# One-hots of the second key on GpSimd, low halves of the gated tiles on VectorE

## The chip, the cores and the metric

The kernel runs on one core of a Trainium2 chip, in one launch. The metric is the time of one execution on the device in microseconds. A profile of one execution shows every instruction of the core's engines: TensorE (PE, and PEld for its weight loads), VectorE (DVE), ScalarE (ACT), GpSimd (POOL) and SyncE (SP), which issues the large transfers.

## What is computed

A network of two blocks in float32 over 256 tokens of 1024 features. The first block (mLSTM, retention, a feed-forward part) and the mixers of the second aren't touched by the change. The change lies in the second block's two PEER layers, cut here to what matters:

```python
q = (x @ w_q).reshape(B, T, PEER_HEADS, 2, PEER_DKEY // 2)
s = jnp.einsum('bthcd,hcnd->bthcn', q, sub_keys)           # 8 heads, 2 sub-keys of 128 each
top_s, top_i = lax.top_k(s, PEER_TOPK)                     # 16 of each
cand_s = top_s[..., 0, :, None] + top_s[..., 1, None, :]
cand_i = top_i[..., 0, :, None] * 128 + top_i[..., 1, None, :]
best_s, pos = lax.top_k(cand_s, PEER_TOPK)
idx = jnp.take_along_axis(cand_i, pos, axis=-1)            # one of 128 x 128 experts
gate = jax.nn.softmax(best_s, axis=-1)
...
h = jax.nn.gelu(jnp.einsum('md,mkd->mk', xb, exp_u[ib]), approximate=False)
return jnp.einsum('mk,mkd->md', gb * h, exp_v[ib])
```

Each token thus picks 8 x 16 = 128 experts (i, j) with a gate each.

## The kernel before

**Dense experts.** The kernel doesn't gather. It computes the hidden value of all 16384 experts for all 256 tokens, multiplies it with a gate that is zero for the experts not chosen, and multiplies by all of `exp_v`. The weights stream through as tiles of 128 x 2048 float32 (1 MB): a "hidden" tile p holds `exp_u` of two values of j with all 128 values of i on the partitions, an "output" tile `exp_v` of two values of j. There are 64 of each per layer. Hidden tiles 0 to 47 come first, then 16 output tiles, then the rest.

**High and low halves.** float32 products are made of three matmuls of a faster type: high x high, high x low, low x high. For each tile ScalarE makes `w_hi` (line 1902), and VectorE (`split_lo`, line 2167) or GpSimd (`lo`, line 1479) makes `w_lo`, the raw tile less `w_hi`. TensorE's `hidden(p)` runs 16 units of three matmuls (lines 1787 to 1789) on a tile. There are two buffers of w_hi and w_lo (three in the first 21 tiles of a layer), so `w_hi` of tile p + 2 waits until TensorE is through with tile p, and `w_lo` follows it. The set `LO_BY_POOL` says which tiles are GpSimd's: 2 to 24, and then every other one from 27 to 47. SP loads tile k when `w_lo` of tile k - 4 is done.

**Gates.** From tile 25 to tile 46 TensorE also makes the gates, in 64 groups of GT = 4 tokens per layer, three groups in a tile (behind units 4, 9 and 15; in tiles 25 and 46 two). For one token the gate matrix over (i, j) is a product of two one-hot matrices with the 128 choices on the partitions: `hot_i` (choice by i) and `hot_j` (choice by j), the latter weighted with the gate value. `gates(g)` (line 1770) runs four such matmuls into one of five PSUM banks. `ijg` holds, with the choices on the partitions, the key i (row 0), the key j (row 1) and the gate value (row 2) of each token. The iota 0 to 127 lies in bank 0 of PSUM for VectorE, and among the constants in SBUF as `cst("iota")`. `hot_i` and `hot_j` have HOT = 3 buffers each.

**Order of the work around the change, written out by hand.** VectorE's `one_hot(g)` (line 2480) compares the iota with `ijg` for four tokens at once, first into `hot_j`, then into `hot_i`, and raises `hot_eq`. GpSimd's `weigh(g)` (line 1484) waits for `hot_eq`, multiplies `hot_j` in place with the gate values and raises `hot_ready`, for which TensorE waits. When a group's gates are there (`gates_done`), VectorE's `apply(g)` (line 2490) multiplies them into the hidden values `hid` of the tiles before, and then calls `one_hot(g + 3)`. ScalarE copies the rest of the gates to `hid` and `staged` (lines 2064, 2068) and raises `gates_read`. In hidden tile n VectorE's queue is: `apply` of the groups in mid-tile, `split_lo(n + 2)` unless GpSimd has it, line 2505 (hidden values of tile n times the gates that are already there), `apply` of the group at the end. GpSimd's queue has for each group of tile p the weighing of three groups ahead, and behind the first of them `lo(p + 1)` if it is its tile. Both engines work strictly in the order of their queues.

Of the kernel before, what the change touches and what calls it, by code (L numbers as in the profile page):

```python
# [9 lines left out]
ALU = mybir.AluOpType  # L10
# [3 lines left out]
P = 128  # L14
# [177 lines left out]

LO_BY_POOL = set(range(2, 25)) | set(range(27, HELD, 2))
LO_COUNT = {}
_counts = {True: 0, False: LAYERS * TILES_A}
for _t in range(TILES_B):
# [998 lines left out]
def second_block(nc, ctx, m, base, erows, ecols, lora_w, side_w, keys, ln_rows, consts_b, spill, out):  # L1198
# [256 lines left out]
    @block.gpsimd  # L1455
    def _(pool):
        pool.dma_start(side_raw[:, :, :], side_w).then_inc(side_loaded, 16)
        pool.dma_start(const_even[:, :], consts_b[:, 0:CONST_EVEN]).then_inc(b_const, 16)
        pool.dma_start(const_rest[:, :], consts_b[:, CONST_EVEN:CONSTS_B]).then_inc(b_const, 16)
        pool.dma_start(lora[:, :], lora_w).then_inc(even_loaded, 16)  # L1460
        pool.dma_start(ecol[:, :], ecols).then_inc(even_loaded, 16)
        pool.dma_start(erow[:, :], erows.partition_broadcast(P)).then_inc(even_loaded, 16)

        def ln_load(n):
            pool.dma_start(ln_rows_at[n][:, 0, :], ln_rows[2 * n].partition_broadcast(P)).then_inc(ln_loaded, 16)
            pool.dma_start(ln_rows_at[n][:, 1, :], ln_rows[2 * n + 1].partition_broadcast(P)).then_inc(ln_loaded, 16)

        pool.wait_ge(tr_lo, 8)
        ln_load(0)
        pool.dma_start(keys_sb, keys[0]).then_inc(keys_loaded, 16)  # L1470

        def peer_layer(layer):

            first, g0 = base + PEER_UV[layer], GROUPS * layer

            def lo(q):
                k = first + q
                pool.wait_ge(hi_ready, k + 1)
                nc.gpsimd.tensor_tensor(lo_of(k), raw[:, k % RAW, :], hi_of(k).bitcast(F32), ALU.subtract).then_inc(lo_pool, 1)  # L1479

            def weigh(g):
                pool.wait_ge(hot_eq, g0 + g + 1)
                at = hot_j[:, g % HOT, :, :]
                nc.gpsimd.tensor_tensor(at, at, ijg[:, 2, g * GT:(g + 1) * GT].unsqueeze(2).broadcast_to([P, GT, KEYS]), ALU.mult).then_inc(hot_ready, 1)  # L1484

            for q in range(FIRST_GATED):
                if q in LO_BY_POOL:
                    lo(q)
            for g in range(HOT):
                weigh(g)  # L1490
            for p in range(FIRST_GATED, LAST_GATED + 1):
                for n, g in enumerate(mid_groups(p) + end_groups(p)):
                    if g + HOT < GROUPS:
                        weigh(g + HOT)
                    if n == 0 and p + 1 in LO_BY_POOL:
                        lo(p + 1)
            pool.wait_ge(gates_done, GROUPS * (layer + 1))
            for b in range(2):
                pool.wait_ge(spilled[b], 16 * (SETS // 2) * (layer + 1))
            ln_load(2 * layer + 1)  # L1500

        peer_layer(0)
        pool.wait_ge(x_ready, normed(1, TT - 1))
        ln_load(2)
        pool.wait_ge(att_lo, 2)
        pool.dma_start(keys_sb, keys[1]).then_inc(keys_loaded, 16)
        peer_layer(1)


    @block.tensor  # L1510
    def _(pe):
# [237 lines left out]
        def peer_layer(layer, split):  # L1749
            transposes(x, 2 * layer)  # L1750
            featured(f"pq{layer}", 0, split=split)
            featured(f"pq{layer}", 1)
            pe.wait_ge(keys_loaded, 16 * (layer + 1))
            wait_read(pe, CHUNK_B[f"pq{layer}", 1])
            for t in range(TT):
                for h in range(PH):
                    last = mm(psum[4 * (1 - t) + h // 2][:, (h % 2) * 2 * KEYS:(h % 2 + 1) * 2 * KEYS], pq[:, h, HALVES[t]], keys_sb[:, h, :],
                              start=True, stop=True)
                last.then_inc(s_done, 1)
            pe.wait_ge(s_read, 2 * layer + 1)  # L1760
            tile, g0, p0, w0 = base + PEER_UV[layer], GROUPS * layer, EXPERT_PAIRS * layer, len(WEIGHED) * layer

            def gates(g):

                pe.wait_ge(hot_ready, g0 + g + 1)
                if g >= len(GATE_BANKS):
                    pe.wait_ge(gates_read, g0 + g + 1 - len(GATE_BANKS))
                dst = psum[GATE_BANKS[g % len(GATE_BANKS)]][:, :].rearrange("p (j t) -> p j t", t=GT)
                for i in range(GT):
                    last = mm(dst[:, :, i], hot_i[:, g % HOT, i, :], hot_j[:, g % HOT, i, :], start=True, stop=True)  # L1770
                last.then_inc(gates_done, 1)

            def hidden(p):

                k = tile + hidden_at(p)
                wait_lo(pe, k)
                if p - 2 in WEIGHED:
                    pe.wait_ge(weighed, w0 + WEIGHED.index(p - 2) + 1)
                elif p > 1:
                    pe.wait_ge(gelu_ready, p0 + p - 1)  # L1780
                wh, wl = hi_of(k), lo_of(k)
                after = dict(GROUPS_IN.get(p, ()))
                for jj in range(2):
                    dst = psum[4 + p % 2][:, jj * S:(jj + 1) * S]
                    for kk_ in range(KD):
                        ws = slice((2 * kk_ + jj) * P, (2 * kk_ + jj + 1) * P)
                        mm(dst, wh[:, ws], act_hi[:, kk_, :], start=kk_ == 0 and jj == 0, stop=False)  # L1787
                        mm(dst, wh[:, ws], act_lo[:, kk_, :], start=False, stop=False)  # L1788
                        last = mm(dst, wl[:, ws], act_hi[:, kk_, :], start=False, stop=kk_ == KD - 1 and jj == 1)  # L1789
                        unit = jj * KD + kk_  # L1790
                        if unit == UNITS - 1:
                            last.then_inc(tile_used, 1)
                        if unit in after:
                            gates(after[unit])

            def output(o):

                k = tile + output_at(o)
                begin, end = o == 0, o == EXPERT_PAIRS - 1
                wait_lo(pe, k)  # L1800
                pe.wait_ge(c_lo_ready, p0 + o + 1)
                wh, wl = hi_of(k), lo_of(k)
                for t in range(TT):
                    for jj in range(2):
                        cs = slice(jj * S + t * P, jj * S + (t + 1) * P)
                        for c in range(2):
                            dst, ws = psum[2 * t + c][:, :], slice(jj * D + c * CW, jj * D + (c + 1) * CW)
                            mm(dst, c_hi[:, o % 2, cs], wh[:, ws], start=begin and jj == 0, stop=False)  # L1808
                            mm(dst, c_hi[:, o % 2, cs], wl[:, ws], start=False, stop=False)  # L1809
                            last = mm(dst, c_lo[:, o % 2, cs], wh[:, ws], start=False, stop=end and jj == 1)  # L1810
                    if end and t == 0:
                        last.then_inc(half_done, 1)
                last.then_inc(tile_used, 1)

            for p in range(HELD):
                hidden(p)
                if p == SELECTED:
                    for t in range(TT):
                        pe.wait_ge(sel_ready, 2 * layer + t + 1)
                        for n in range(3):  # L1820
                            last = nc.tensor.transpose(psum[6 + t][:, n * P:(n + 1) * P], sel[:, t, n, :], ident)
                        last.then_inc(sel_t, 1)
                    pe.wait_ge(ijg_ready, 2 * layer + 2)
                    pe.wait_ge(s_read, 2 * layer + 2)
            pe.wait_ge(gates_read, g0 + GROUPS)
            for o in range(EARLY):
                output(o)
            for p in range(HELD, EXPERT_PAIRS):
                hidden(p)
            for o in range(EARLY, EXPERT_PAIRS):  # L1830
                output(o)
# [325 lines left out]
    def _(dve):  # L2157
# [260 lines left out]
        def peer_layer(layer, t0):  # L2418
# [55 lines left out]
            def one_hot(g):  # L2474
# [1 line left out]
                if g >= HOT:  # L2476
                    dve.wait_ge(gates_done, g0 + g + 1 - HOT)
                tok = slice(g * GT, (g + 1) * GT)
                for keys_at, dst in ((1, hot_j), (0, hot_i)):
                    ins = V.tensor_tensor(dst[:, g % HOT, :, :], bcast(psum[0][:, 0:KEYS].unsqueeze(1), [P, GT, KEYS]),  # L2480
                                          bcast(ijg[:, keys_at, tok].unsqueeze(2), [P, GT, KEYS]), ALU.is_equal)
                ins.then_inc(hot_eq, 1)

            def apply(g):

# [347 lines left out]
```

## Time and profile before

| | |
|---|---|
| median of 3 runs | 3635.1 us (3630.31 to 3638.41) |
| the profiled execution's own time | 3633.8 us |
| its span in the profile | 3632.0 us |
| TensorE matmul busy | 3286.6 us (90%) |
| VectorE busy | 2188.9 us (60%) |
| ScalarE busy | 1503.1 us (41%) |
| GpSimd busy | 535.3 us (15%) |
| mean granted TensorE clock | 0.943 |

The gated tiles lie at about 1897 to 2123 us (first PEER layer) and 2941 to 3164 us (second). Times in the trace are microseconds from the start of the span; the busy time of an engine is the sum of its instructions' times, and "idle before, <-releaser" is how long the engine stood still before an instruction and what ended that. The granted clock is TensorE's, as a share of 2.4 GHz.

### The profile page before, as it was taken

To read this page: it belongs to the slowest core of one execution; us is meant where nothing else is said; L and a number is where in the kernel's file an instruction comes from. 1 tells how busy PE (TensorE), PEld (TensorE's weight loads), DVE (VectorE), ACT (ScalarE), POOL (GpSimd) and SP (SyncE) were. 2 spreads that over 40 slices of the span, in tenths; PEclk is the share of its full clock that TensorE was granted. 3 is DMA by queue.
4 is the path that set the end of the run, shared out by engine and by line. 5 is a ranking of instruction groups with operands and counts; after the bars stand their busy time and mean duration, and the time that the engine had idled before them with its cause. 6 is when DMAs were issued, how large, how long until landed. Compare 5 with 4: busy or idle time off the path is not lost.

```text
span 3632.0 us, 49546 instructions
## 1 busy us (share of the span) xinstructions
PE 3286.6 (90%) x20440; PEld 2901.1 (80%) x20440; DVE 2188.9 (60%) x3110; ACT 1503.1 (41%) x1681; POOL 535.3 (15%) x275
## 2 busy tenths in 40 slices
PE   6899999799998998777998899999848988999998
PEld 6787789587877986666998889888638988889886
DVE  4766655566665554745786655555665966654555
ACT  5443444453444444401434344444334443344443
POOL 0000000000000000000566620000001856500000
PEclk9999999889999998877999999999969999999999
DMA  4444545334545553202443355555403533465553
GB/s 181 152 174 170 204 153 186 139 119 160 194 159 174 183 185 145 96 2 71 169 157 121 122 201 206 186 188 191 164 35 135 185 131 112 157 233 184 188 185 127
DMA packets 87677, 565.23 MB, mean 156 GB/s; under 512 B 10176, under 2 KB 10192, under 8 KB 23584
## 3 DMA queue, kind: packets, MB, share of 16 engines
q1 hardware_dynamic: 80496, 534.81, 40.8%
q0 software_dynamic: 6960, 27.27, 2.2%
q8 instruction: 163, 2.67, 0.3%
q14 instruction: 58, 0.48, 0.0%
HBM read 552.61 MB, written 9.44 MB: 155 GB/s over the span
## 4 chain that ended last, share of the span: by engine, by line
PE 43%; DVE 4%; POOL 4%; ACT 3%; issue 1%; ACTq 0%; DVEq 0%
PE bank L1810 7%; PE bank L1808 6%; PE bank L1809 6%; PE bank L1787 6%; PE bank L1788 6%; PE bank L1789 6%; POOL w_lo L1479 3%; ACT w_hi L1902 2%; PE bank L1770 1%; PE bank L1534 1%; PE bank L1535 1%; PE bank L1536 1%; DVE hot_i L2480 1%; POOL hot_j L1484 1%; DVE hot_j L2480 1%
## 5 line engine op out<-in xcount | busy, mean ns | idle before, releaser
L1902 ACT ACTIVATE w_hi<-raw 128x2048 fp32r<-128x2048 f32 x290 | 555.5, 1916 | 844.2 <-PE bank L1810 395.5
L2167 DVE TENSOR_TENSOR w_lo<-raw,w_hi 128x2048 fp32r<-128x2048 f32 x222 | 531.7, 2396 | 614.2 <-ACT w_hi L1902 614.0
L874 DVE TENSOR_TENSOR w_lo<-raw,w_hi 128x2048 fp32r<-128x2048 f32 x202 | 462.6, 2292 | 409.7 <-ACT w_hi L686 406.0
L1787 PE MATMUL bank<-act_hi,w_hi 128*128 128x256 f32 x2048 | 600.8, 293 | 60.8 <-POOL w_lo L1479 55.2
L686 ACT ACTIVATE w_hi<-raw 128x2048 fp32r<-128x2048 f32 x202 | 386.8, 1916 | 542.9 <-PE bank L463 369.8
L1788 PE MATMUL bank<-act_lo,w_hi 128*128 128x256 f32 x2048 | 588.3, 287 | 0.0
L1789 PE MATMUL bank<-act_hi,w_lo 128*128 128x256 f32 x2048 | 587.4, 287 | 0.0
L1787 PEld LDWEIGHTS bank<-act_hi,w_hi 128*128 128x128 f32 x2048 | 400.8, 196 | 66.4 <-POOL w_lo L1479 60.2
L1808 PE MATMUL bank<-w_hi,c_hi 128*128 128x512 f32 x1024 | 405.0, 396 | 0.0
L1809 PE MATMUL bank<-w_lo,c_hi 128*128 128x512 f32 x1024 | 405.0, 395 | 0.0
L1810 PE MATMUL bank<-w_hi,c_lo 128*128 128x512 f32 x1024 | 405.0, 395 | 0.0
L1788 PEld LDWEIGHTS bank<-act_lo,w_hi 128*128 128x128 f32 x2048 | 401.6, 196 | 0.1
L1789 PEld LDWEIGHTS bank<-act_hi,w_lo 128*128 128x128 f32 x2048 | 401.3, 196 | 0.0
L1479 POOL TENSOR_TENSOR w_lo<-raw,w_hi 128x2048 fp32r<-128x2048 f32 x68 | 322.0, 4739 | 195.9 <-ACT w_hi L1902 195.6
L497 PE MATMUL bank<-act_hi,w_hi 128*128 128x256 f32 x1024 | 297.8, 291 | 14.4 <-DVE act_lo L921 8.5
L498 PE MATMUL bank<-act_lo,w_hi 128*128 128x256 f32 x1024 | 296.0, 289 | 0.0
L499 PE MATMUL bank<-act_hi,w_lo 128*128 128x256 f32 x1024 | 295.6, 289 | 0.0
L461 PE MATMUL bank<-w_hi,act_hi 128*128 128x512 f32 x576 | 236.9, 411 | 26.5 <-DVE w_lo L874 22.3
L462 PE MATMUL bank<-w_lo,act_hi 128*128 128x512 f32 x576 | 230.0, 399 | 0.0
L1810 PEld LDWEIGHTS bank<-w_hi,c_lo 128*128 128x128 f32 x1024 | 192.4, 188 | 46.7
L463 PE MATMUL bank<-w_hi,act_lo 128*128 128x512 f32 x576 | 229.5, 399 | 0.0
L1808 PEld LDWEIGHTS bank<-w_hi,c_hi 128*128 128x128 f32 x1024 | 192.4, 188 | 46.4 <-issue 0.3
(482 smaller groups left out, 5758.2 us busy)
## 6 DMA issues: line engine op xcount, KB each, us to landing
raw<-weights SPq DMA_DIRECT2D x492, 1024.0 KB, 4.8
row<-rows POOLq DMA_DIRECT2D x48, 256.0 KB, 4.0
spill<-staged SPq DMA_DIRECT2D x32, 256.0 KB, 3.9
hid<-spill SPq DMA_DIRECT2D x32, 256.0 KB, 4.8
y<-w_pe POOLq DMA_DIRECT2D x2, 1024.0 KB, 5.1
ln_row_mix<-ln_rows POOLq DMA_DIRECT2D x4, 512.0 KB, 4.6
hid<-keys POOLq DMA_DIRECT2D x2, 1024.0 KB, 6.1
ln_row_ffn<-ln_rows POOLq DMA_DIRECT2D x4, 512.0 KB, 7.3
```

Of the source, the lines that this page charges most:

```text
L497: nc.tensor.matmul(dst, wh, hi[:, ki, :], start=ki == 0 and f % 2 == 0, stop=False)
L686: nc.scalar.activation(w_hi[:, k % SPLIT, :], raw[:, k % RAW, :], ACT.Copy).then_inc(hi_ready, 1)
L874: nc.vector.tensor_tensor(w_lo[:, k % SPLIT, :], raw[:, k % RAW, :], w_hi[:, k % SPLIT, :].bitcast(F32), ALU.subtract).then_inc(lo_ready, 1)
L1479: nc.gpsimd.tensor_tensor(lo_of(k), raw[:, k % RAW, :], hi_of(k).bitcast(F32), ALU.subtract).then_inc(lo_pool, 1)
L1787: mm(dst, wh[:, ws], act_hi[:, kk_, :], start=kk_ == 0 and jj == 0, stop=False)
L1788: mm(dst, wh[:, ws], act_lo[:, kk_, :], start=False, stop=False)
L1789: last = mm(dst, wl[:, ws], act_hi[:, kk_, :], start=False, stop=kk_ == KD - 1 and jj == 1)
L1808: mm(dst, c_hi[:, o % 2, cs], wh[:, ws], start=begin and jj == 0, stop=False)
L1809: mm(dst, c_hi[:, o % 2, cs], wl[:, ws], start=False, stop=False)
L1810: last = mm(dst, c_lo[:, o % 2, cs], wh[:, ws], start=False, stop=end and jj == 1)
L1902: A.activation(hi_of(k), raw[:, k % RAW, :], ACT.Copy).then_inc(hi_ready, 1)
L2167: V.tensor_tensor(lo_of(k), raw[:, k % RAW, :], hi_of(k).bitcast(F32), ALU.subtract).then_inc(lo_ready, 1)
```

## The change

GpSimd no longer takes any `w_lo` of the gated tiles: `LO_BY_POOL` ends at tile 24, and VectorE makes the low half of tiles 25 to 47. GpSimd no longer weighs what VectorE compared. For each token of a group it runs one tensor-scalar instruction of 128 x 128: iota equal to the token's key j, times the gate value, both read as one scalar per partition from `ijg`. It starts when `ijg` is there and then waits only for the buffer (`gates_done` of three groups before). VectorE compares for `hot_i` alone. TensorE waits for `hot_eq` (now VectorE's `hot_i`) and for `hot_ready` (GpSimd's `hot_j`).

```diff
-LO_BY_POOL = set(range(2, 25)) | set(range(27, HELD, 2))
+LO_BY_POOL = set(range(2, 25))
...
-            def weigh(g):
-                pool.wait_ge(hot_eq, g0 + g + 1)
-                at = hot_j[:, g % HOT, :, :]
-                nc.gpsimd.tensor_tensor(at, at, ijg[:, 2, g * GT:(g + 1) * GT].unsqueeze(2).broadcast_to([P, GT, KEYS]), ALU.mult).then_inc(hot_ready, 1)
+            def weighed_hot(g):
+
+                if g >= HOT:
+                    pool.wait_ge(gates_done, g0 + g + 1 - HOT)
+                for i in range(GT):
+                    tok = g * GT + i
+                    last = nc.gpsimd.tensor_scalar(hot_j[:, g % HOT, i, :], cst("iota"), ijg[:, 1, tok:tok + 1], ijg[:, 2, tok:tok + 1],
+                                                   ALU.is_equal, ALU.mult)
+                last.then_inc(hot_ready, 1)
...
-            for g in range(HOT):
-                weigh(g)
-            for p in range(FIRST_GATED, LAST_GATED + 1):
-                for n, g in enumerate(mid_groups(p) + end_groups(p)):
-                    if g + HOT < GROUPS:
-                        weigh(g + HOT)
-                    if n == 0 and p + 1 in LO_BY_POOL:
-                        lo(p + 1)
+            pool.wait_ge(ijg_ready, 2 * layer + 2)
+            for g in range(GROUPS):
+                weighed_hot(g)
...
             def gates(g):
 
+                pe.wait_ge(hot_eq, g0 + g + 1)
                 pe.wait_ge(hot_ready, g0 + g + 1)
...
-                for keys_at, dst in ((1, hot_j), (0, hot_i)):
-                    ins = V.tensor_tensor(dst[:, g % HOT, :, :], bcast(psum[0][:, 0:KEYS].unsqueeze(1), [P, GT, KEYS]),
-                                          bcast(ijg[:, keys_at, tok].unsqueeze(2), [P, GT, KEYS]), ALU.is_equal)
-                ins.then_inc(hot_eq, 1)
+                V.tensor_tensor(hot_i[:, g % HOT, :, :], bcast(psum[0][:, 0:KEYS].unsqueeze(1), [P, GT, KEYS]),
+                                bcast(ijg[:, 0, tok].unsqueeze(2), [P, GT, KEYS]), ALU.is_equal).then_inc(hot_eq, 1)
```

## Rows read from the trace of the kernel before

**Rows 1.** The page: busy times, and the chain by line.

```profile
PE 3286.6 (90%) x20440; PEld 2901.1 (80%) x20440; DVE 2188.9 (60%) x3110; ACT 1503.1 (41%) x1681; POOL 535.3 (15%) x275
...
PE bank L1810 7%; PE bank L1808 6%; PE bank L1809 6%; PE bank L1787 6%; PE bank L1788 6%; PE bank L1789 6%; POOL w_lo L1479 3%; ACT w_hi L1902 2%; PE bank L1770 1%; PE bank L1534 1%; PE bank L1535 1%; PE bank L1536 1%; DVE hot_i L2480 1%; POOL hot_j L1484 1%; DVE hot_j L2480 1%
```

**Rows 2.** Windows of ungated tiles and of gated tiles.

```profile
core 0: us, PE busy (x) PEld busy (x) DVE busy (x) ACT busy (x) POOL busy (x), PEclk, DMA share, GB/s
1897.00:1918.70 21.70, 19.59 (x167) 19.39 (x165) 10.13 (x17) 9.32 (x16) 9.33 (x7) 1.00 0.20 74
1918.70:1938.00 19.30, 17.07 (x144) 16.88 (x144) 12.62 (x22) 7.83 (x18) 12.78 (x8) 1.00 0.37 138
1978.20:1999.20 21.00, 18.59 (x144) 18.40 (x144) 13.49 (x22) 7.58 (x18) 12.72 (x8) 0.92 0.31 114
2061.30:2083.90 22.60, 19.85 (x144) 19.66 (x144) 14.54 (x22) 7.27 (x18) 12.72 (x8) 0.86 0.29 106
2105.40:2123.00 17.60, 17.57 (x138) 17.57 (x139) 10.54 (x17) 5.66 (x17) 10.74 (x5) 0.91 0.38 140
1755.00:1850.00 95.00, 95.00 (x798) 95.00 (x798) 91.07 (x334) 41.80 (x35) 80.90 (x18) 1.00 0.52 183
1918.70:2105.40 186.70, 163.89 (x1296) 162.18 (x1296) 123.81 (x190) 67.57 (x162) 114.78 (x64) 0.94 0.34 122
2962.80:3150.00 187.20, 164.23 (x1314) 162.52 (x1315) 127.22 (x193) 67.91 (x164) 117.94 (x65) 0.95 0.34 126
```

**Rows 3.** Waits, 1903 to 2112 us: total us, times, longest.

```profile
PE bank L1787 <- POOL w_lo L1479: 25.0, 10, 2.8
```

**Rows 4.** The chain in order of time, around one wait: start, us, what.

```profile
1951.60 0.32 DVE hid L2490
1951.91 0.60 DVE hot_j L2480
1952.51 0.61 DVE hot_i L2480
...
1953.19 1.04 POOL hot_j L1484
1954.23 4.52 POOL w_lo L1479
...
1958.79 0.39 PE bank L1787
...
1960.85 0.89 PE bank L1770 x8
```

**Rows 5.** Timeline of TensorE: full clock, then behind a wait.

```profile
1885.22 0.28 PE L1787 MATMUL bank<-act_hi,w_hi 128*128 128x256 f32 x1
1885.58 0.28 PE L1787 MATMUL bank<-act_hi,w_hi 128*128 128x256 f32 x1
...
1978.24 0.39 PE L1787 MATMUL bank<-act_hi,w_hi 128*128 128x256 f32 x1 [2.38 <-POOL w_lo L1479]
...
1979.25 0.41 PE L1787 MATMUL bank<-act_hi,w_hi 128*128 128x256 f32 x1
...
1979.89 0.41 PE L1787 MATMUL bank<-act_hi,w_hi 128*128 128x256 f32 x1
```

**Rows 6.** Instructions of GpSimd and of VectorE's w_lo, by tile and line.

```profile
L1484 POOL TENSOR_TENSOR hot_j<-hot_j,ijg x128: 1040/1042/3107, 1895.4 to 3155.3; 128x512 f32<-128x512 f32 x128
...
L1479 POOL TENSOR_TENSOR w_lo<-raw,w_hi x68: 4520/4627/6682, 1753.7 to 3157.7; 128x2048 fp32r<-128x2048 f32 x68
...
L2167 DVE TENSOR_TENSOR w_lo<-raw,w_hi x222: 2285/2293/3800, 1423.5 to 3611.2; 128x2048 fp32r<-128x2048 f32 x111
...
L2827 POOL MEMSET const-float32-1.0<- 128x1 f32 x1 | 0.1, 99 | 0.0
```

**Rows 7.** Timeline of GpSimd, VectorE and ScalarE, 1953 to 1961 us.

```profile
1954.19 4.55 POOL L1479 TENSOR_TENSOR w_lo<-raw,w_hi 128x2048 fp32r<-128x2048 f32 x1
1958.70 3.09 POOL L1484 TENSOR_TENSOR hot_j<-hot_j,ijg 128x512 f32<-128x512 f32 x1
...
1953.82 0.68 DVE L2480 TENSOR_TENSOR hot_j<-bank,ijg 128x512 f32<-128x512 f32 x1
1954.42 0.68 DVE L2480 TENSOR_TENSOR hot_i<-bank,ijg 128x512 f32<-128x512 f32 x1
1957.65 3.24 DVE L2167 TENSOR_TENSOR w_lo<-raw,w_hi 128x2048 fp32r<-128x2048 f32 x1 [2.55 <-ACT w_hi L1902]
...
1955.70 1.91 ACT L1902 ACTIVATE w_hi<-raw 128x2048 fp32r<-128x2048 f32 x1 [1.31 <-PE bank L1789]
```

**Rows 8.** VectorE's gating instructions, 1903 to 2112 us: busy, mean ns.

```profile
L2490 DVE TENSOR_TENSOR hid<-bank,hid 128x208 f32<-128x208 f32 (+20 forms) x60 | 26.6, 444 | 13.4 <-PE bank L1770 13.1
L2505 DVE TENSOR_TENSOR hid<-bank,hid 128x8 f32<-128x8 f32 (+19 forms) x20 | 8.0, 398 | 31.2 <-ACT hid L2056 31.2
```

## The prediction

> **What bounds the kernel now.** I read the page's busy shares first [rows 1]: TensorE is busy for 90% of the span, no other engine for more than 60%. TensorE is therefore the path nearly everywhere, and the change can only pay where TensorE stands still or runs at a lower clock. The chain that ended last, by line, names one thing that is no TensorE work and belongs to the change: `w_lo` by GpSimd on line 1479, 3% of the span [rows 1].
>
> Next the table of windows [rows 2]. In the ungated expert tiles TensorE is busy all the time (95.00 of 95.00 us). In the gated tiles, two tiles at a time, it is not: a pair takes 19.30 us with 17.07 us of matmuls at full clock, or 21.00 us and 22.60 us where the granted clock fell to 0.92 and 0.86. The nine pairs of layer 0 take 186.70 us, and the same stretch of layer 1 takes 187.20 us. The reader is to see two losses: a wait of some 2.3 us in each pair, and after most of these waits matmuls at the lower level.
>
> The waits of TensorE in that stretch have one releaser: GpSimd's `w_lo`, 25.0 us in 10 waits [rows 3]. The chain in order of time shows why it is late [rows 4]. The tile's high half had long been made, but GpSimd's queue holds the weighing of a one-hot ahead of the subtraction, and that weighing waits for VectorE's two comparisons, which wait for VectorE's gating of `hid`. Weighing (1.04) and `w_lo` (4.52) then run one after the other and the matmul starts 0.04 us later. Half of the tiles (those whose low half VectorE makes) never make TensorE wait [rows 3].
>
> The clock: the matmul on line 1787 repeats every 0.36 us at full clock, and every 0.64 us behind such a wait, 0.41 us long each instead of 0.28 [rows 5]. That is the step from 2.4 GHz to 1.2 GHz: TensorE had stood still 2.38 us just before.
>
> **What the change does, part by part.**
>
> *The low halves of 11 tiles per layer go from GpSimd to VectorE.* GpSimd loses 11 times 4.5 us [rows 6]. VectorE takes a tile in 2.29 us, the median of its row [rows 6]. VectorE starts it right behind `w_hi`: in the trace 1955.70 + 1.91 gives 1957.61, and VectorE starts at 1957.65 [rows 7]. Counted from the end of the tile whose buffer it takes, the low half is there 0.3 + 1.9 + 2.3 = 4.5 us later, and TensorE needs it one tile later, 8.5 us (17.07 / 2). That leaves 4.0 us.
>
> *VectorE makes one comparison per group instead of two.* It loses 64 of 680 ns, start to start 0.60 us, per layer [rows 7], and gains the 11 `w_lo`. Per tile it then has 2.29 for `w_lo`, 0.17 to 0.67 for line 2505 (0.40 mean), three gatings of 0.44 and three comparisons of 0.60: 5.8 us of 8.5 us [rows 7, 8]. It is no bound, and the time is covered.
>
> *GpSimd makes the second key's weighted one-hots alone.* Per group it loses one tensor-tensor of 128x512 at 1.04 us [rows 6] and gets four tensor-scalar instructions of 128x128. No row of before shows GpSimd doing a tensor-scalar. From below a token costs no less than GpSimd's shortest instruction, 0.10 us for a 128x1 memset; from above I take 1.04 us, the whole 128x512 instruction. Nearest is a quarter of the 512-wide one, 0.26 us, plus one fixed part of 0.10 us: 0.36 us, which I take. Per group that is 1.44 us, per tile of three groups 4.3 us.
>
> The Trainium skill, GPSIMD Engine Reference, sections 7 and 3.1, speaks against such small instructions: some 102 cycles for each read command, not overlapped with the one before, and at best about 1.8 cycles an element. With the data and two scalar columns that gives an estimate of 3 x 85 ns + 192 ns = 0.45 us a token. No trace here shows it. By it a tile would cost GpSimd 12 x 0.45 + 2.29 = 7.7 us, still under 8.5, so the sum would be the same with less room.
>
> *The lock between the two engines.* `w_lo` on VectorE and GpSimd's instructions exclude each other [rows 7]: VectorE's started at 1957.65, GpSimd's `w_lo` ended at 1958.74, VectorE ended 2.2 us behind that, at 1960.89, and the weighing that GpSimd had ready at 1958.70 took 3.09 us instead of 1.04. The comparison with PSUM at 1954.42 ran at its usual 0.68 us under GpSimd's `w_lo`. So after the change GpSimd is shut out for 2.29 us in every tile, and VectorE waits for at most one token (0.36 us, where it waits about 1.0 us now). GpSimd per tile: 12 x 0.36 + 2.29 = 6.6 us of 8.5. It is covered by TensorE's work, with 1.9 us to spare. With HOT = 3 the one-hots are asked for one whole tile ahead, so bursts within a tile even out.
>
> *The waits.* TensorE gets one more wait per group, on `hot_eq`. Behind it queue the four gate matmuls and the rest of the tile. VectorE's comparison is issued a tile ahead, and is now earlier by one comparison and by GpSimd's 1.04, so I cost it at nothing. GpSimd's waits on `gates_done` hold back nothing but later one-hots, since it has no `w_lo` left behind them. SP's loads wait for `w_lo` of four tiles before; those come earlier, never later.
>
> **The sum.** Nine pairs of layer 0: 186.70 less 9 x 17.07 gives 33.1 us [rows 2]. The tiles in front: 21.70 less 19.59, 2.1 us. The last two tiles, with no wait in them but the clock at 0.91: 17.60 us against 2 x 16 x 0.36 + 5 x 0.89 = 16.0 us [rows 2, 4, 5], 1.6 us. Together 36.8 us a layer, and the second layer has the same stretch (187.20), so 74 us. The profiled execution took 3633.8 us (span 3632.0, 1.8 around it). 3633.8 - 74 = 3560; the median of the runs, 3635.1, is 1.3 higher, so I say **3561 us**. If nothing overlapped at the ends of a pair, it would be 2 x 5.76 + 6 x 0.89 = 16.9 instead of 17.07, another 4 us; if the clock still falls sometimes, some 1.5 to 3 us each time.
>
> **The rivals.**
>
> *GpSimd becomes the bound, and the kernel is slower.* TensorE is held up once 12 t + 2.29 is over 8.54, at t = 0.52 us a token. The mean gated tile of before takes 186.70 / 18 = 10.37 us, so it pays until 12 t + 2.29 = 10.37: t = 0.67 us decides. At t = 0.80 a tile is 11.9 us, and 21.3 tiles a layer times two times 1.5 us gives 3700; at the upper bound 1.04 a tile is 14.8 us and the time 3823. For it: two scalars per partition and two operations in one instruction that no row shows. Against it: the row of 512 elements, where four tokens' worth of data costs 1.04 in all, so that t = 0.67 would need over 0.4 us of fixed cost. Chance 16%.
>
> *GpSimd is the bound, but less slow than now* (t between 0.52 and 0.66): at 0.60 a tile is 9.5 us and the time 3635 - 43 x 0.88 = 3597, in all 3563 to 3628. Chance 15%.
>
> *VectorE's `w_lo` is locked out by a train of tokens* rather than by one. Then it comes up to 4.3 us late where 4.0 are free, with the clock falling in some tiles: 0.5 to 1 us a tile, 3582 to 3603. Rows 7 speak against it: GpSimd had the next instruction ready, and VectorE went first all the same. The Trainium skill, SBUF — State Buffer, section "Who interferes with whom", says that issue order decides who blocks; by that rule VectorE goes next, as in the trace. Chance 5%.
>
> *It does nothing that can be measured*, since t happens to be near 0.67: 4%.
>
> **How the numbers follow.** TensorE as the bound has 60%, its own range 3550 to 3575. The range that leaves no more than 2 in 10 out takes this and the cases where GpSimd or the lock costs something but not all, up to no change: 3546 to 3642. Less than 0.2% (7 us) can't be told from no change. Faster: 60 + 15 + 5 = 80%; same 4%; slower 16%.
>
> **What would show it.** In the profile of the changed kernel: TensorE's waits in the gated tiles gone, pairs at 17 us with the clock at 1.00; VectorE's `w_lo` at 2.3 to 2.7 us in all gated tiles; a token on GpSimd at 0.3 to 0.4 us, GpSimd busy 50 to 80% there and idle on `gates_done` of TensorE. Wrong it would be if TensorE's gate matmuls wait for `hot_j` by GpSimd, with GpSimd never idle; then the start-to-start of two tokens is the number to read. If TensorE's first matmul of a tile waits for VectorE's `w_lo`, the lock was mis-sized.

## The result: slower by 1.1%, and the profile after

The changed kernel takes 3674.8 us (median of 4 runs, 3671.66 to 3676.93) against 3632.95 us for the kernel before; the ratio is 1.0113, with a 95% interval of 1.0095 to 1.013. The forecast was 3561 us. The profiled execution took 3671.66 us, with a span of 3670.0 us.

The page of the changed kernel, busy times and the chain by line, beside [rows 1]:

```profile
PE 3296.1 (90%) x20440; PEld 2905.1 (79%) x20440; DVE 2140.9 (58%) x3004; ACT 1502.0 (41%) x1681; POOL 744.7 (20%) x637
...
PE bank L1808 6%; PE bank L1809 6%; PE bank L1810 6%; PE bank L1787 6%; PE bank L1788 6%; PE bank L1789 6%; PE bank L1770 3%; ACT w_hi L1902 1%; PE bank L1533 1%; PE bank L1535 1%; PE bank L1534 1%; POOL w_lo L1478 1%; PE bank L1557 0%; PE bank L1558 0%; PE bank L1559 0%
```

GpSimd's `w_lo` has gone from 3% of the chain to 1% (the ungated tiles), as it should. GpSimd itself is busy 209 us longer, and the gate matmuls on line 1770 have grown from 1% to 3% of the chain. The window of [rows 2] that held nine pairs of tiles, and the one behind it:

```profile
core 0: us, PE busy (x) PEld busy (x) DVE busy (x) ACT busy (x) POOL busy (x), PEclk, DMA share, GB/s
1918.70:2105.40 186.70, 153.57 (x1201) 149.58 (x1200) 94.53 (x136) 61.77 (x151) 186.70 (x199) 0.95 0.32 113
2105.40:2139.00 33.60, 27.56 (x217) 26.86 (x216) 17.36 (x23) 11.49 (x30) 30.11 (x32) 0.95 0.33 115
```

GpSimd is busy for all of the 186.70 us, and TensorE runs 1201 matmuls in them where it ran 1296 before. TensorE's waits in the gated tiles of layer 0 (1918.7 to 2140 us: total, times, longest), beside [rows 3]:

```profile
PE bank L1770 <- issue: 32.3, 21, 2.3
PE bank L1770 <- DVE hot_i L2479: 6.9, 6, 1.3
```

The waits for `w_lo` are gone. In their place TensorE waits in front of a gate matmul. "issue" means that the profile names no releaser; the timeline shows one such wait (TensorE, then GpSimd):

```profile
1926.93 0.28 PE L1789 MATMUL bank<-act_hi,w_lo 128*128 128x256 f32 x1
1929.49 1.13 PE L1770 MATMUL bank<-hot_j,hot_i 128*128 128x128 f32 x8 [2.28 <-issue]
...
1929.38 0.79 POOL L1486 TENSOR_SCALAR hot_j<-const_rest,ijg 128x128 f32<-128x128 f32 x1
```

The matmul begins 0.11 us after GpSimd has gone on to the next group's first token. VectorE's `hot_i` for that group had been made 7.8 us before (1921.0 to 1921.7). The six waits that the profile puts down to `hot_i` are the same wait under another name. The longest of them:

```profile
1943.64 1.13 PE L1770 MATMUL bank<-hot_j,hot_i 128*128 128x128 f32 x8 [1.29 <-DVE hot_i L2479]
...
1943.52 0.79 POOL L1486 TENSOR_SCALAR hot_j<-const_rest,ijg 128x128 f32<-128x128 f32 x1
...
1935.19 0.68 DVE L2479 TENSOR_TENSOR hot_i<-bank,ijg 128x512 f32<-128x512 f32 x1
```

This matmul is the gates of group 12 of the layer (counted from 0), and the last row is that group's `hot_i`: done at 1935.87, 7.8 us before. GpSimd's last token for the group ended 0.10 us before the matmul, when GpSimd went on to the next one (1943.52). It is so at all 27 waits of the layer: GpSimd's last token of the group ended 0.10 us before the matmul, and the group's `hot_i` 6.9 to 9.2 us before. So all of them, 39.2 us, are waits for GpSimd.

GpSimd's timeline (start, us) shows a queue that never stands still, 240 tokens in 227.53 us:

```profile
1892.90 10.09 POOL L1486 TENSOR_SCALAR hot_j<-const_rest,ijg 128x128 f32<-128x128 f32 x12 [3.74 <-ACT ijg L2110]
1904.23 3.55 POOL L1486 TENSOR_SCALAR hot_j<-const_rest,ijg 128x128 f32<-128x128 f32 x4 [1.24 <-PE bank L1770]
1907.99 227.53 POOL L1486 TENSOR_SCALAR hot_j<-const_rest,ijg 128x128 f32<-128x128 f32 x240 [0.21 <-PE bank L1770]
```

The tokens by tile, and VectorE's `w_lo` in the gated tiles of layer 0, beside [rows 6] (min/median/max in ns):

```profile
L1486 POOL TENSOR_SCALAR hot_j<-const_rest,ijg x512: 780/786/2926, 1892.9 to 3196.6; 128x128 f32<-128x128 f32 x171
...
L2167 DVE TENSOR_TENSOR w_lo<-raw,w_hi x22: 2291/2294/2380, 1902.4 to 2131.0; 128x2048 fp32r<-128x2048 f32 x22
```

A token takes 0.786 us, not 0.36. GpSimd's 240 tokens without a pause are 20 tiles of three groups, and they take 11.38 us each (227.53 / 20), where a tile took 10.37 us before.

### The profile page after: what moved, and what is told of

The parts are those of the page before. It is cut to its first block, busy times and chain, and to the rows that moved or that the text cites. A ratio compares the mean times of both kernels' runs of the same rounds, so it can differ in the third digit from the quotient of the medians.

```text
span 3670.0 us, 49812 instructions
## 1 busy us (share of the span) xinstructions
PE 3296.1 (90%) x20440; PEld 2905.1 (79%) x20440; DVE 2140.9 (58%) x3004; ACT 1502.0 (41%) x1681; POOL 744.7 (20%) x637
## 4 chain that ended last, share of the span: by engine, by line
PE 46%; DVE 3%; issue 3%; ACT 2%; POOL 1%; DVEq 0%; ACTq 0%
PE bank L1808 6%; PE bank L1809 6%; PE bank L1810 6%; PE bank L1787 6%; PE bank L1788 6%; PE bank L1789 6%; PE bank L1770 3%; ACT w_hi L1902 1%; PE bank L1533 1%; PE bank L1535 1%; PE bank L1534 1%; POOL w_lo L1478 1%; PE bank L1557 0%; PE bank L1558 0%; PE bank L1559 0%
## 5 line engine op out<-in xcount | busy, mean ns | idle before, releaser
L2167 DVE TENSOR_TENSOR w_lo<-raw,w_hi 128x2048 fp32r<-128x2048 f32 x244 | 560.4, 2297 | 696.5 <-ACT w_hi L1902 696.3
L873 DVE TENSOR_TENSOR w_lo<-raw,w_hi 128x2048 fp32r<-128x2048 f32 x202 | 462.6, 2292 | 410.2 <-ACT w_hi L685 406.5
L1486 POOL TENSOR_SCALAR hot_j<-const_rest,ijg 128x128 f32<-128x128 f32 x512 | 482.3, 954 | 10.4 <-ACT ijg L2110 7.5
L1478 POOL TENSOR_TENSOR w_lo<-raw,w_hi 128x2048 fp32r<-128x2048 f32 x46 | 221.9, 4831 | 191.3 <-ACT w_hi L1902 191.0
```

What stands on the lines that cost most here:

```text
L873: nc.vector.tensor_tensor(w_lo[:, k % SPLIT, :], raw[:, k % RAW, :], w_hi[:, k % SPLIT, :].bitcast(F32), ALU.subtract).then_inc(lo_ready, 1)
L1486: last = nc.gpsimd.tensor_scalar(hot_j[:, g % HOT, i, :], cst("iota"), ijg[:, 1, tok:tok + 1], ijg[:, 2, tok:tok + 1], ALU.is_equal, ALU.mult)
L2167: V.tensor_tensor(lo_of(k), raw[:, k % RAW, :], hi_of(k).bitcast(F32), ALU.subtract).then_inc(lo_ready, 1)
```

## The experiments

All times are medians; the ratios are to the kernel before, on the same chip (its medians were 3635.8 us for experiments 1, 4, 5 and 8, 3636.7 us for 2, 6, 7 and 9, and 3637.2 us for 3 and 10).

**1. What a token costs, by itself.** After the first PEER layer GpSimd runs extra instructions on constants, writing to a buffer that is free then; ScalarE waits for the last of them. Nothing else is changed; the single run took 3670.75 us.

```diff
         ln_load(2)
+        for at in range(0, 48, 16):
+            last = nc.gpsimd.tensor_scalar(probe[:, at:at + 16], const_rest[:, 0:16], const_rest[:, 5:6], const_rest[:, 6:7], ALU.is_equal, ALU.mult)
...  (the same with 64, 128, 256, 512 columns, and 128 columns in other forms)
+        last.then_inc(probed, 1)
```

> The changed kernel with a row of extra GpSimd instructions in its idle time between the two PEER layers: the token instruction in 16, 64, 128, 256 and 512 columns, and 128 columns with two immediates, with one operation, with multiply and add, as a copy and as a product of two tensors. Theory F (a fixed part of each instruction makes the 0.78 us): 16 columns take 0.6 us or more and 512 columns under 1.5 us. Rival E (each element is dear because of the two operations): 16 columns take about 0.1 us, 64 about 0.4, 512 about 3.1 us. Rival S (the two scalars read per partition are dear): with immediates 128 columns take under half of 0.78 us.

By line of the kernel with the probe: count, min/median/max in ns (a maximum far off the median is an instruction that stood behind a VectorE instruction with two SBUF inputs). Lines 1508 to 1516 are equal-and-multiply with two scalars per partition, 16 to 512 columns. Then 128 columns: 1518 with two immediates, 1520 with equal alone, 1522 with multiply and add. 1524 is a copy, and 1526 and 1528 are products of two tensors.

```profile
L1508 POOL TENSOR_SCALAR rel<-const_rest x3: 411/412/428, 2606.9 to 2607.7; 128x16 f32<-128x16 f32 x3
L1510 POOL TENSOR_SCALAR rel<-const_rest x3: 567/568/568, 2608.1 to 2609.2; 128x64 f32<-128x64 f32 x3
L1512 POOL TENSOR_SCALAR rel<-const_rest x3: 782/782/2519, 2609.8 to 2611.3; 128x128 f32<-128x128 f32 x3
L1514 POOL TENSOR_SCALAR rel<-const_rest x2: 1209/1210/1210, 2613.8 to 2615.0; 128x256 f32<-128x256 f32 x2
L1516 POOL TENSOR_SCALAR rel<-const_rest x1: 2067/2067/2067, 2616.2 to 2616.2; 128x512 f32<-128x512 f32 x1
L1518 POOL TENSOR_SCALAR rel<-const_rest x3: 641/642/1359, 2618.4 to 2620.5; 128x128 f32<-128x128 f32 x3
L1520 POOL TENSOR_SCALAR rel<-const_rest x3: 597/603/2707, 2621.2 to 2622.4; 128x128 f32<-128x128 f32 x3
L1522 POOL TENSOR_SCALAR rel<-const_rest x3: 434/437/443, 2625.1 to 2625.9; 128x128 f32<-128x128 f32 x3
L1524 POOL COPY rel<-const_rest x3: 296/469/482, 2626.3 to 2627.2; 128x128 f32<-128x128 f32 x3
L1526 POOL TENSOR_TENSOR rel<-const_rest x3: 460/462/465, 2627.4 to 2628.3; 128x128 f32<-128x128 f32 x3
L1528 POOL TENSOR_TENSOR rel<-const_rest x1: 1515/1515/1515, 2628.7 to 2628.7; 128x512 f32<-128x512 f32 x1
```

None of the three expectations fits. From 16 to 512 columns the time of equal-and-multiply grows by (2067 - 412) / 496 = 3.34 ns a column, which leaves 0.36 us fixed: 0.36 + 128 x 3.34 ns = 0.79 us. So over half of a token is per-column work, and nearly half is fixed. The compare is what is dear in it: multiply and add with the same operands takes 437 ns, 345 ns less, and equal alone, a single operation, still takes 603 ns. The two per-partition scalars are worth 140 ns. The 1515 ns of line 1528 is not a price: the instruction began at 2628.69, while a VectorE instruction with two SBUF inputs ran until 2629.06.

**2. The token's duration alone.** One line of the changed kernel. `hot_j` is then no one-hot; every instruction, wait and operand stays.

```diff
-                                                   ALU.is_equal, ALU.mult)
+                                                   ALU.mult, ALU.add)
```

> The changed kernel with one word changed in the token instruction: multiply and add in place of equal and multiply (hot_j is then no one-hot; everything else, the two scalars and 128 columns too, stays). In the probe this form takes 0.44 us where the compare takes 0.78. Theory (the token's duration alone makes the change slow): 12 x 0.44 + 1.95 = 7.2 us a tile, under TensorE's 8.5: 3560 to 3570 us, and no wait for hot_j. Rival (the number of small instructions, their waits or the added wait for hot_eq make it slow): over 3600 us.

3563.9 us, ratio 0.980 (0.9784 to 0.9817). The token takes 453 ns (median), and GpSimd's timeline has a pause in every tile, in which it waits for TensorE:

```profile
1939.16 7.23 POOL L1486 TENSOR_SCALAR hot_j<-const_rest,ijg 128x128 f32<-128x128 f32 x12 [1.17 <-PE bank L1770]
1947.56 7.23 POOL L1486 TENSOR_SCALAR hot_j<-const_rest,ijg 128x128 f32<-128x128 f32 x12 [1.17 <-PE bank L1770]
```

What to read here is the 8.40 us from start to start: that is TensorE's own pace in a gated tile, and the twelve tokens, with one `w_lo` of VectorE among them, fit into 7.23 us. With only the token's time changed, the kernel is 111 us faster than the changed one. Apart from the time that each token itself takes, number, order and waits of the small instructions cost nothing that can be measured: this kernel is within 2 us of two others that have no tokens at all (experiments 5 and 10).

**3. A token between the two.** Equal alone, without the gate value (`hot_j` is an unweighted one-hot).

```diff
-... cst("iota"), ijg[:, 1, tok:tok + 1], ijg[:, 2, tok:tok + 1], ALU.is_equal, ALU.mult)
+... cst("iota"), ijg[:, 1, tok:tok + 1], None, ALU.is_equal)
```

> The changed kernel with one operation in the token instruction: equal, without the gate value (hot_j is an unweighted one-hot). The probe gives this form 0.60 us. If GpSimd's tokens set the pace as 12 t + 1.95, a tile takes 9.2 us where TensorE needs 8.54 (at 0.44 us a token it was TensorE's, at 0.78 it was 11.3): 42.7 tiles x 0.6 = 27 us over the 3564 us that TensorE allows, 3585 to 3597 us. Rival (something else in the compare form, or a threshold near 0.7): 3565 us.

3578.2 us, ratio 0.9838 (0.9822 to 0.9855). The direction is right, but the kernel is 14 us above the 3564 of experiment 2, half of the 27 us expected, and outside the expected range.

```profile
L1486 POOL TENSOR_SCALAR hot_j<-const_rest,ijg x512: 592/599/2740, 1898.0 to 3104.6; 128x128 f32<-128x128 f32 x171
...
1913.08 178.25 POOL L1486 TENSOR_SCALAR hot_j<-const_rest,ijg 128x128 f32<-128x128 f32 x240 [1.06 <-PE bank L1770]
```

The first row is the token by tile, the second GpSimd's timeline. GpSimd is again without a pause over 240 tokens, 8.91 us a tile. The expectation had set this against 8.54 us and 42.7 tiles. It has to be set against TensorE's 8.40 us and 20 tiles a layer, and GpSimd starts each layer with three groups made ahead: see the table under experiment 4.

**4. The lock** (GpSimd standing still while VectorE makes a `w_lo` from two SBUF inputs). VectorE's instruction on the gated tiles gets one SBUF input instead of two. The low halves of 44 tiles are left out (what is written there is the raw tile less a constant); the instruction takes 2287 ns as before.

```diff
+                gated = any(FIRST_GATED < k - base - first <= LAST_GATED + 1 for first in PEER_UV)
+                other = bcast(psum[0][:, 0:1], [P, TW]) if gated else hi_of(k).bitcast(F32)
-                V.tensor_tensor(lo_of(k), raw[:, k % RAW, :], hi_of(k).bitcast(F32), ALU.subtract)...
+                V.tensor_tensor(lo_of(k), raw[:, k % RAW, :], other, ALU.subtract)...
```

> The changed kernel, but VectorE's instruction on the gated tiles takes the raw tile less one PSUM column in place of the high half, so that it has a single SBUF input (the low halves of 44 tiles are thereby left out). Theory: in the changed kernel GpSimd's 12 tokens of 0.79 us plus 1.8 us of lock set the tile at 11.3 us; without the lock 9.4 us, so 42.7 tiles give back 80 us: 3595 us. Rival: the lock is no part of it, and the time stays at 3675 us.

3591.5 us, ratio 0.988 (0.9864 to 0.9897): 83 us back. The longest token falls from 2926 to 1577 ns, and 240 tokens take 185.72 us:

```profile
1912.21 185.72 POOL L1486 TENSOR_SCALAR hot_j<-const_rest,ijg 128x128 f32<-128x128 f32 x240 [0.65 <-PE bank L1770]
```

In the changed kernel 21 of VectorE's `w_lo` start in GpSimd's 227.53 us. So the lock costs GpSimd (227.53 - 185.72) / 21 = 2.0 us for each of them, and costs VectorE nearly nothing (2291 to 2380 ns in the changed kernel).

With experiments 2 to 4 the pace of GpSimd in a tile can be set beside the time of the kernel. TensorE needs 8.40 us, and the kernel that it bounds takes 3564 us:

| kernel | GpSimd's tile | over 8.40, x 40 tiles | measured over 3564 |
|---|---|---|---|
| multiply and add | 7.23 us | 0 | 0 us |
| equal alone | 8.91 us | 20 us | 14 us |
| no lock | 9.29 us | 35 us | 28 us |
| changed kernel | 11.38 us | 119 us | 111 us |

Each measured number lies 6 to 8 us below the product, 3 to 4 us a layer, which fits the three groups made ahead at the start of each layer (argued, not tried on its own).

**5. One half of the change: low halves only.** One-hots and weighing as in the kernel before.

```diff
-LO_BY_POOL = set(range(2, 25)) | set(range(27, HELD, 2))
+LO_BY_POOL = set(range(2, 25))
```

> The kernel before with only the low halves moved to VectorE; one-hots and weighing as before. Theory (the late low half on GpSimd was the whole loss, and GpSimd's tokens alone made the change slow): VectorE per tile 2.3 + 0.4 + 3 x 1.64 = 7.6 us, with up to 1 us for the lock 8.6 us, at TensorE's 8.5 us: 3560 to 3575 us. Rival (VectorE with both comparisons and all low halves becomes the bound, with its 2.5 us idle wait for the high half in each tile): 10 us or more a tile, 3620 to 3650 us.

3564.7 us, ratio 0.9808 (0.9792 to 0.9824). TensorE never waits for an operand in the gated tiles and stays at the upper level of its clock, with VectorE busy 85% of the window:

```profile
core 0: us, PE busy (x) PEld busy (x) DVE busy (x) ACT busy (x) POOL busy (x), PEclk, DMA share, GB/s
1918.70:2073.00 154.30, 154.22 (x1319) 153.82 (x1318) 131.19 (x199) 68.18 (x163) 56.88 (x55) 1.00 0.41 148
```

This line alone gives all that the forecast counted on. It is faster than both kernels.

**6. The other half: tokens only.** GpSimd keeps every other `w_lo`, with tokens in place of weighings.

```diff
 (the changed kernel)
-LO_BY_POOL = set(range(2, 25))
+LO_BY_POOL = set(range(2, 25)) | set(range(27, HELD, 2))
-            for g in range(GROUPS):
-                weighed_hot(g)
+            for g in range(HOT):
+                weighed_hot(g)
+            for p in range(FIRST_GATED, LAST_GATED + 1):
+                for n, g in enumerate(mid_groups(p) + end_groups(p)):
+                    if g + HOT < GROUPS:
+                        weighed_hot(g + HOT)
+                    if n == 0 and p + 1 in LO_BY_POOL:
+                        lo(p + 1)
```

> The other half of the change alone: GpSimd makes the tokens and keeps the low half of every other gated tile, VectorE compares for hot_i alone. Theory: GpSimd per pair of tiles 24 x 0.786 + 4.55 + 1.95 = 25.4 us against 20.74 before: 10.7 pairs, two layers, 99 us slower, 3735 us. Rival (tokens overlap with something): about 3675 us.

3723.3 us, ratio 1.0241 (1.0224 to 1.0258), 12 us below the 3735 us expected. A pair of tiles now takes GpSimd 25.1 us:

```profile
1975.29 20.69 POOL L1486 TENSOR_SCALAR hot_j<-const_rest,ijg 128x128 f32<-128x128 f32 x24
1995.96 4.49 POOL L1478 TENSOR_TENSOR w_lo<-raw,w_hi 128x2048 fp32r<-128x2048 f32 x1
2000.44 20.62 POOL L1486 TENSOR_SCALAR hot_j<-const_rest,ijg 128x128 f32<-128x128 f32 x24
```

The two halves don't add up: 71 us less and 87 us more would make 16 us more, and the change cost 42 us. What a half is worth depends on what bounds the kernel beside it. Next to the tokens the low halves are worth 12.6 - 11.4 = 1.2 us of GpSimd's tile, 48 us in 40 tiles (3723.3 against 3674.8), and not 71; next to VectorE's low halves the tokens cost 110 us (3674.8 against 3564.7), and not 87.

**7. Two tokens of four on VectorE.** The changed kernel, with `for i in range(GT // 2)` on GpSimd and, on VectorE:

```diff
+                for i in range(GT // 2, GT):
+                    at = g * GT + i
+                    V.tensor_scalar(hot_j[:, g % HOT, i, :], psum[0][:, 0:KEYS], ijg[:, 1, at:at + 1], ijg[:, 2, at:at + 1], ALU.is_equal, ALU.mult)
```

> The changed kernel with two of a group's four tokens made by VectorE (from the iota in PSUM, 0.32 us start to start each). Theory: GpSimd 6 x 0.786 + 1.95 = 6.7 us, VectorE 2.3 + 0.4 + 3 x (0.44 + 0.6 + 0.64) = 7.7 us a tile, both under 8.5: 3560 to 3575 us. Rival: VectorE's part makes hot_j late, 3600 us or more.

3566.7 us, ratio 0.9807 (0.9791 to 0.9824). As expected: halving GpSimd's tokens is enough.

**8. All tokens on VectorE,** low halves of every other tile on GpSimd, which has nothing else then. The kernel before with the same `V.tensor_scalar` for all four tokens, and no weighing.

> Tokens on VectorE instead of GpSimd: for each token one tensor-scalar from the iota in PSUM, equal and times the gate; GpSimd makes only the low halves of every other tile, as before. Theory: a token costs VectorE about 0.2 us, so 3 x (4 x 0.2 + 0.6 + 0.44) + 0.4 + half of 2.3 = 7.1 us a tile; GpSimd's low half starts right behind the high half and is there in 4.5 + 2.2 us: TensorE bound, 3560 us. Rival (a fixed part makes each token on VectorE 0.4 us): 9.4 us a tile, 3600 us.

3582.1 us, ratio 0.9858 (0.9841 to 0.9876). It lies between the theory (3560) and the rival (3600). The token's price was taken too low here too: the rival's 0.4 us is what one takes. A token takes 401 ns (0.32 us start to start) and VectorE is busy for 157.44 of 171.30 us. TensorE waits 6 times for its `hot_i` in each layer, 5.0 us, and each of these matmuls starts 0.05 to 0.06 us after VectorE has made it; so VectorE is at times the bound (the token by tile, then a window):

```profile
L2467 DVE TENSOR_SCALAR hot_j<-bank,ijg x512: 394/401/408, 1895.6 to 3102.6; 128x128 f32<-128x128 f32 x171
...
1918.70:2090.00 171.30, 166.30 (x1400) 163.99 (x1399) 157.44 (x371) 69.87 (x173) 41.59 (x10) 1.00 0.40 143
```

**9 and 10. The order of GpSimd's queue in the kernel before.** First the low half ahead of all weighings of its tile, then ahead of the last weighing of the tile before as well.

```diff
 (9)
-                for n, g in enumerate(mid_groups(p) + end_groups(p)):
+                if p + 1 in LO_BY_POOL:
+                    lo(p + 1)
+                for g in mid_groups(p) + end_groups(p):
                     if g + HOT < GROUPS:
                         weigh(g + HOT)
-                    if n == 0 and p + 1 in LO_BY_POOL:
-                        lo(p + 1)
 (10)
+                for g in mid_groups(p):
+                    if g + HOT < GROUPS:
+                        weigh(g + HOT)
+                if p + 2 in LO_BY_POOL and p < LAST_GATED:
+                    lo(p + 2)
+                for g in end_groups(p):
+                    if g + HOT < GROUPS:
+                        weigh(g + HOT)
```

> The kernel before, with only the order of GpSimd's queue changed: in each tile the low half first, then the weighings. Theory (the low half was late because of its place behind the weighing, not because GpSimd is slow): it is there 0.3 + 1.9 + 4.6 = 6.8 us after the tile before, and is needed at 8.5: 3560 to 3570 us. Rival (the weighings behind it come too late for the gate matmuls): 3600 us or more, with waits for hot_j.

3589.6 us, ratio 0.9872 (0.9855 to 0.9888): two thirds of the gain, not all, and between the two expectations. The chain in order of time shows why: the high half is done at 1948.56, but ahead of the low half stands the weighing for the group at the end of the tile before, which waited for VectorE and ends at 1952.06. Ten waits of 1.0 us remain.

```profile
1946.64 1.92 ACT w_hi L1902
...
1951.02 1.04 POOL hot_j L1484
1952.06 4.54 POOL w_lo L1479
1956.64 0.39 PE bank L1787
```

TensorE's waits of this kernel, 1903 to 2095 us:

```profile
PE bank L1787 <- POOL w_lo L1479: 9.8, 10, 1.3
```

> The kernel before with the low half placed one step further ahead in GpSimd's queue than in low_first: ahead of the weighing for the group at the end of the tile before, which waits for VectorE's w_lo and gating. In low_first that weighing ended 2.4 us after the high half was there. Theory (place in the queue is all): the last 1.0 us waits of TensorE go too, 3560 to 3570 us. Rival (the weighing now comes behind 4.6 us of subtraction and is late for the gate matmul): 3585 us or more.

3565.9 us, ratio 0.9804 (0.9787 to 0.982), and in the window TensorE is busy throughout:

```profile
1918.70:2073.00 154.30, 154.30 (x1325) 154.30 (x1324) 113.42 (x193) 67.71 (x165) 99.13 (x66) 1.00 0.43 148
```

GpSimd could thus have kept its low halves. They were late by their place in its queue.

## Why the prediction was wrong

The step that failed is the price of a token: "Nearest is a quarter of the 512-wide one, 0.26 us, plus one fixed part of 0.10 us: 0.36 us, which I take." It measured 0.786 us, between the bounds of 0.10 and 1.04 that the text gave, and above the 0.67 us at which, by its own rival, the kernel becomes slower. The row it was taken from was of another operation. In the probe GpSimd's compare costs far more than its multiply (equal-and-multiply 782 ns, multiply-and-add 437 ns), and the fixed part of the equal-and-multiply instruction is 0.36 us, not 0.10. Even the row's own operation, a product of two tensors, takes 462 ns in 128 columns there. So 0.10 us of the 0.43 missing is the scaling from 512 to 128 columns, and the rest is that the token is another instruction. The estimate from the Trainium skill, GPSIMD Engine Reference, sections 7 and 3.1, 0.45 us, was closer and still short by 0.34 us; the measurement decides. The argument against the rival, that t = 0.67 would need over 0.4 us fixed cost, left out that the operation's own price could differ.

Point by point:

- *The loss in the kernel before, 74 us.* Right. Three kernels with no wait in the gated tiles (experiments 2, 5 and 10) take 3563.9 to 3565.9 us, 71 to 73 us less than before; TensorE then has the window to itself at clock 1.00.
- *VectorE can take all low halves.* Right, and with more on its hands than forecast: in experiment 5 it also makes both comparisons, and still TensorE doesn't wait.
- *VectorE's comparison for `hot_i` and the added wait cost nothing.* Right. Experiment 2 has no wait of TensorE, and the 6.9 us that carry `hot_i`'s name in the changed kernel are waits for GpSimd's last token, as the rows at 1943 us show.
- *The lock, 2.29 us per tile for GpSimd and at most one token for VectorE.* Nearly right: 2.0 us, and at most 0.1 us for VectorE. The rival of a train of tokens that locks VectorE out fell: its longest `w_lo` in the gated tiles of layer 0 is 2380 ns.
- *GpSimd's tile, 12 t + 2.29, against 8.54, and what it gives in time.* The form held. TensorE's own tile was 8.40 us. With the measured t it gives 12 x 0.786 + 2.29 = 11.7 us and, by the text's own 42.7 tiles over 10.37 us, 3693 us, where 3675 was measured; with the 2.0 us lock 11.4 us, and 3680. The case that came is the first rival, given 16%.

## What to carry to other kernels

Before moving an elementwise operation to GpSimd, time that very operation in that very size in one throwaway run: a row of another operation on the same amount of data was off by a factor of two. Where an engine's result comes late, look first at what stands ahead of it in its queue and what that waits for; here one reordering, or one line that moves the late work to an engine with room, brought all of the 2%, and the other half of the change took it away and more. Of two edits that come together, price each alone at the stage's pace-setter, and don't add the prices: here they would have made 16 us where 42 came.

## What the hardware showed that I had not expected

- On GpSimd a float32 tensor-scalar with equal and multiply took 0.36 us plus 3.34 ns a column; 128 columns took 782 ns, with equal alone 603, with two immediates 642, with multiply and add 437. So the kind of operation matters as much as the size.
- The lock between VectorE and GpSimd is one-sided for the tokens: behind GpSimd's 4.5 us `w_lo` VectorE waited about 1 us [rows 7], but with GpSimd full of 0.79 us tokens VectorE's `w_lo` waited at most 0.1 us (2380 against 2291 ns), while GpSimd lost 2.0 us each time. In layer 0 of the changed kernel 14 of 22 `w_lo` start 0.01 to 0.02 us after a token, which then takes 2.9 us. Six others start 0.35 to 0.38 us into a token: they take 2.29 us all the same, that token its usual 0.78 us, and only the next one 2.5 us. The Trainium skill, SBUF — State Buffer, section "Terms", has the pair held for the full instruction; for the tokens the trace differs, since a wait of some 0.4 us would then be seen in those six.
- It isn't the shortness of the token. In the probe the 512-column token instruction (2616.22 to 2618.29) and a `w_lo` of VectorE from 2616.93 on ran side by side for 1.36 us; `w_lo` took its usual 2.29 us, and the token instruction lies on the line of the shorter ones. Under the 512-column product of two tensors (2628.69 to 2630.20) a VectorE instruction with two SBUF inputs took 1514 ns and ended at 2630.49; the same line took 505 ns 2.4 us earlier. So the kind of GpSimd's instruction seems to decide; this rests on one case of each.

```profile
2616.22 2.07 POOL L1516 TENSOR_SCALAR rel<-const_rest 128x512 f32<-128x512 f32 x1
...
2616.93 2.29 DVE L2194 TENSOR_TENSOR w_lo<-raw,w_hi 128x2048 fp32r<-128x2048 f32 x1 [3.75 <-ACT w_hi L1928]
...
2628.69 1.51 POOL L1528 TENSOR_TENSOR rel<-const_rest 128x512 f32<-128x512 f32 x1
...
2628.98 1.51 DVE L2600 TENSOR_TENSOR qidx<-qidx,rtmp 128x256 f32<-128x256 f32 x1
```

- VectorE needed 0.40 us (0.32 start to start) for the same token from PSUM, half of GpSimd's time.
